# Recurrent heads of a hybrid decoder step: two chain links per round, the prompt's group normalisation in the later rounds, the state products on four row groups

## What is computed

```python
def step(st, inp):
    r_t, w_t, k_t, v_t, kk_t, b_t = inp
    sa = jnp.einsum('bhvk,bhk->bhv', st, -kk_t)
    st = st * w_t[:, :, None, :] + sa[..., None] * b_t[:, :, None, :] + v_t[..., None] * k_t[:, :, None, :]
    return st, jnp.einsum('bhvk,bhk->bhv', st, r_t)
st_final, ys = lax.scan(step, state0.astype(F32), xs)
y = jnp.swapaxes(ys, 0, 1)
mean = jnp.mean(y, axis=-1, keepdims=True)
var = jnp.mean(jnp.square(y - mean), axis=-1, keepdims=True)
y = ((y - mean) * lax.rsqrt(var + RWKV_GN_EPS)).reshape(B, S, RWKV_WIDTH)
y = y * gn_g.astype(F32) + gn_b.astype(F32)
bonus = jnp.sum(rf * kf * r_k.astype(F32), axis=-1, keepdims=True) * vf
out = ((y + bonus.reshape(B, S, RWKV_WIDTH)) * g.astype(F32)).astype(p.dtype)
```

## Time and profile before

| | us |
|---|---|
| time, median of 3 runs | 2107.24 (2105.16 to 2107.76) |
| span of the profiled execution | 2100.0 |
| the same execution with what lies around its span, taken as the median | 2107.24 |
| PE busy | 1898.0 (90%) |
| DVE busy | 704.1 (34%) |
| ACT busy | 510.4 (24%) |
| rounds of the recurrent heads | 431.53 to 497.79 |
| tail of the recurrent heads | 497.79 to 525.51 |
| next block's first transfer | 526.72 |

### The profile page before, as it was taken

The page is one execution under the profiler, slowest core; times in us unless marked ns, Lnnn a source line. Parts: engine busy times, 40 slices in busy tenths (PEclk is TensorE's granted clock), DMA queues, the critical chain, the costliest instruction groups (busy, mean ns, idle before and its releaser), DMA issues. The chain is left out here.

```text
span 2100.0 us, 38294 instructions
## 1 busy us (share of the span) xinstructions
PE 1898.0 (90%) x15868; PEld 1287.9 (61%) x15868; DVE 704.1 (34%) x1349; ACT 510.4 (24%) x861; POOL 139.8 (7%) x180
## 2 busy tenths in 40 slices
PE   6999996798879989989897999999999999999993
PEld 6999985766565558978644554544554554455441
DVE  4447758323535544446433111111111111111111
ACT  4446632232122223254222111101110111111111
POOL 0000000400023310000100000000000000000000
PEclk8999997788899999999997999999999999999997
DMA  8545531111233429524669999999999999999996
GB/s 225 142 126 134 140 74 23 24 41 28 108 104 108 136 76 290 141 101 126 231 272 372 415 422 424 427 423 395 407 423 426 421 423 404 409 424 422 422 426 217
DMA packets 210765, 543.62 MB, mean 259 GB/s; under 512 B 44536, under 2 KB 168538, under 8 KB 183632
## 3 DMA queue, kind: packets, MB, share of 16 engines
q1 hardware_dynamic: 202274, 532.97, 66.7%
q0 software_dynamic: 7936, 8.68, 2.0%
q10 hardware_dynamic: 438, 0.32, 0.1%
HBM read 524.86 MB, written 28.59 MB: 264 GB/s over the span
## 5 line engine op out<-in xcount | busy, mean ns | idle before, releaser
L2774 PE MATMUL p_u<-w_expert,xgT 128*64 128x256 f32 x2048 | 241.4, 390 | 32.5 <-DMA w_expert<-in_w_up_dram 32.4
L2774 PE MATMUL p_g<-w_expert,xgT 128*64 128x256 f32 x2048 | 231.9, 379 | 0.9 <-DVE xgT L2854 0.9
L2774 PEld LDWEIGHTS p_u<-w_expert,xgT 128*64 128x64 f32 x2048 | 149.3, 140 | 117.3 <-DMA w_expert<-in_w_up_dram 42.0
L2790 PE MATMUL p_y<-w_expert,hidT 128*64 128x512 f32 x960 | 219.2, 599 | 0.5 <-DVE hidT L2866 0.5
L2774 PEld LDWEIGHTS p_g<-w_expert,xgT 128*64 128x64 f32 x2048 | 147.2, 137 | 88.0 <-issue 18.8
L2742 PE MATMUL p_xg<-low,slot_sel 128*64 128x512 f32 x768 | 179.5, 603 | 5.2 <-DVE slot_sel L2838 5.2
L2790 PEld LDWEIGHTS p_y<-w_expert,hidT 128*64 128x64 f32 x960 | 66.7, 137 | 126.7 <-issue 125.9
L2859 DVE CAST row<-rowf 128x1 int32<-128x1 f32 x32 | 4.9, 154 | 357.4 <-POOLq L2949 357.4
L2909 ACT ACTIVATE act_g<-p_g 128x256 f32<-128x256 f32 x32 | 12.3, 384 | 429.6 <-PE p_u L2774 429.6
L2946 POOL DMA_INDIRECT x_dram<-y_slots,row x32 | 49.9, 1559 | 974.4 <-DVE y_slots L2870 974.4
L2742 PEld LDWEIGHTS p_xg<-low,slot_sel 128*64 128x64 f32 x768 | 52.9, 138 | 85.7 <-issue 75.4
(11 more groups left out here) (571 smaller groups left out, 2633.0 us busy)
## 6 DMA issues: line engine op xcount, KB each, us to landing
w_expert<-in_w_gate_dram SPq DMA_DIRECT2D x64, 2048.0 KB, 22.0
w_expert<-in_w_up_dram SPq DMA_DIRECT2D x64, 2048.0 KB, 23.2
w_expert<-in_w_down_dram SPq DMA_DIRECT2D x60, 2048.0 KB, 20.4
w_in_raw<-in_w_in_dram SPq DMA_DIRECT2D x32, 1024.0 KB, 5.7
lat<-in_cache_kv_latent_dram SPq DMA_DIRECT2D x128, 128.0 KB, 2.1
ho_raw<-in_w_out_dram SPq DMA_DIRECT2D x12, 1024.0 KB, 6.4
tables_sb<-in_w_out_dram SPq DMA_DIRECT2D x4, 1024.0 KB, 7.7
mem_k_s<-in_cache_mem_k_dram SPq DMA_DIRECT2D x8, 512.0 KB, 7.3
```

Source lines behind the costliest of these rows:

```text
L2774: mm = pe.matmul(acc[SL * h:SL * h + SL, 0:FF // 2], xgT[:, t, g // 2, :], w[g][:, FF * t + FF // 2 * h:FF * t + FF // 2 * h + FF // 2], s ...
L2790: mm = pe.matmul(p_y[SL * h:SL * h + SL, 512 * b:512 * b + 512], hidT[:, j, g, :], tile, start=(g == 0 and j == 0), stop=(g == 1 and j == 1))
```

## The change

1. **Two links per round.** `CHAIN` gives each round two links: round 0 has link 1, rounds 1 to 3 have links 2 and 3, 4 and 5, 6 and 7, and the later ones none. Each link's outputs go with it. The second link stands behind the outputs of the first, its outputs behind `states`.
2. **Normalisation spread.** From round 4 (`FIN_ROUND`) to round 7 each round normalises the prompt's 256 columns of two pairs (piece p = c - 4, 512 columns): `centre(p)` at the start of the round, `spread(p)` (sums of squares) before `states`, `inverses(p)` behind them. The transposes of the prompt's end state stand at the start of round 4. Piece 4, the samples' 64 columns of all eight pairs, is left for the tail.
3. **State products.** In `states` the four `b_exp` products (both n, both h) are issued first, then the four `k_exp` products, then the eight products with old states of n = 0 and of n = 1.
4. **Gates.** `gates(j)` makes the 320 columns of one pair; pairs 0 to 4 in rounds 1 to 5, 5 and 6 in round 6, 7 in round 7 (`GATES`).
5. ACT's eight additions of the bias (L1124) go in twos to rounds 0 to 3 instead of all to round 0. `cen` and `inv_g` become five buffers each. `head_uses` follows the new order.

The diff, cut:

```diff
+CHAIN = [(1, 0), (2, 3), (4, 5), (6, 7)] + [(0, 0)] * 5
+FIN_ROUND = 4
+GATES = [(), (0,), (1,), (2,), (3,), (4,), (5, 6), (7,), ()]
...
                     for n in range(2):
                         free(pe, ("st", j, n))
+                    for left, right in ((XS[:, :, 0:64], b_exp), (rowsS["v"], k_exp)):
+                        for n in range(2):
+                            for h in range(2):
+                                gg, hk = slice(64 * h + 32 * n, 64 * h + 32 * n + 32), slice(64 * h, 64 * h + 64)
+                                pe.matmul(B(("st", j, n))[hk, 0:288], left[gg, j, :], right[gg, j, :, :].rearrange("p b n -> p (b n)"), start=(right is b_exp), stop=False)
+                    for n in range(2):
                         empty_of(pe, "V", ("mts", j, n))
-                        for h in range(2):
-                            gg, hk = slice(64 * h + 32 * n, 64 * h + 32 * n + 32), slice(64 * h, 64 * h + 64)
-                            out = B(("st", j, n))
-                            pe.matmul(out[hk, 0:288], XS[gg, j, 0:64], b_exp[gg, j, :, :].rearrange("p b n -> p (b n)"), start=True, stop=False)
-                            pe.matmul(out[hk, 0:288], rowsS["v"][gg, j, :], k_exp[gg, j, :, :].rearrange("p b n -> p (b n)"), start=False, stop=False)
...
+                def gates(j):
+                    free(pe, ("gate", j))
+                    pe.wait_ge(g2_in, 16)
+                    for t in range(2):
+                        ins = pe.matmul(B(("gate", j))[:, 0:T], gate_w(t, j), sg[:, t, :], start=(t == 0), stop=(t == 1))
                     ins.then_inc(filled, 1)
+                def finals():
+                    empty_of(pe, "V", ("ch", NCH - 1))
...
+                def centre(p):
+                    free(pe, ("cen", p))
+                    if p == 4:
+                        empty_of(pe, "A", ("st", HP - 1, 1))
+                    else:
+                        empty_of(pe, "V", ("yp", NCH - 1))
+                    pe.matmul(B(("cen", p))[:, :], S.table("centre"), piece(y, p), start=True, stop=True).then_inc(filled, 1)
+                def spread(p):
+                    free(pe, ("gs", p))
+                    empty_of(pe, "A", ("cen", p))
+                    for e in range(8):
+                        ins = pe.matmul(B(("gs", p))[0:64, 2 * e:2 * e + 2], sqg[:, 512 * p + 64 * e:512 * p + 64 * e + 64], S.table("headsum")[:, 0:128:64], start=True, stop=True)
+                    ins.then_inc(filled, 1)
+                def inverses(p):
+                    free(pe, ("gi", p))
+                    pe.wait_ge(g_inverted, p + 1)
+                    for e in range(8):
+                        for h in range(2):
+                            ins = pe.matmul(B(("gi", p))[64 * h:64 * h + 64, 64 * e:64 * e + 64], inv_g[p][:, 2 * e + h:2 * e + h + 1].to_broadcast([64, 64]), ident[0:64, 0:64], start=True, stop=True)
+                    ins.then_inc(filled, 1)
                 for c in range(HP + 1):
-                    if 1 <= c < NCH:
-                        chain(c)
+                    first, second = CHAIN[c]
+                    p = c - FIN_ROUND if FIN_ROUND <= c < HP else None
+                    if c == FIN_ROUND:
+                        finals()
+                    if p is not None:
+                        centre(p)
+                    if first and c >= 1:
+                        chain(first)
                     if c < HP:
                         maps(c)
-                    if 1 <= c < NCH:
-                        outputs(c)
+                    if first and c == 0:
+                        chain(first)
+                    if first:
+                        outputs(first)
+                    if second:
+                        chain(second)
+                    if p is not None:
+                        spread(p)
                     if c >= 1:
                         states(c - 1)
+                    if second:
+                        outputs(second)
+                    if p is not None:
+                        inverses(p)
+                    for j in GATES[c]:
+                        gates(j)
+                centre(4)
+                spread(4)
+                inverses(4)
...
+                def squares(p):
+                    full_of(act, ("cen", p))
+                    done(act.activation(sqg[:, 512 * p:512 * p + 512], B(("cen", p))[:, :], ACT.Square))
+                def roots(p):
+                    full_of(act, ("gs", p))
+                    done(act.activation(inv_g[p], B(("gs", p))[0:64, 0:16], ACT.Sqrt, bias=gn_eps[:, :], scale=1.0 / HD))
...
+                def normalise(p):
+                    full_of(dve, ("gi", p))
+                    empty_of(dve, "V", ("cen", p))
+                    done(dve.tensor_tensor(cen[p], cen[p], B(("gi", p))[:, :], ALU.mult))
+                    dve.wait_ge(biased, HP)
+                    empty_of(dve, "V", ("gi", p))
+                    js = (2 * p, 2 * p + 1) if p < 4 else range(HP)
+                    ts = slice(0, SEQ) if p < 4 else slice(SEQ, T)
+                    for i, j in enumerate(js):
+                        x = cut(cen[p], p)[:, i, :]
+                        dve.scalar_tensor_tensor(x, x, S.vec('gn_g')[:, j:j + 1], k[:, j, ts], ALU.mult, ALU.add).then_inc(scaled, 1)
+                    empty_of(dve, "A", ("gate", js[-1]))
+                    dve.wait_ge(scaled, 2 * p + len(js))
+                    dve.tensor_tensor(piece(S.r, p), cut(cen[p], p), piece(gate, p), ALU.mult)
```

More of the change, by code:

```diff
@@ L1026, in _ @@
[L1026 to L1044, removed]
-                    for c, (o, w) in enumerate(CHUNKS):
-                        free(pe, ("gi", q, c))
-                        for e in range(o // 64, (o + w) // 64):
-                            for h in range(2):
-                                ins = pe.matmul(B(("gi", q, c))[64 * h:64 * h + 64, 64 * e - o:64 * e - o + 64], inv_g[q][:, 2 * e + h:2 * e + h + 1].to_broadcast([64, 64]), ident[0:64, 0:64], start=True, stop=True)
-                        ins.then_inc(filled, 1)
@@ L1253, in _, with link, output @@
-                normalise(0)
-                scale(0)
-                normalise(1)
-                scale(1)
+                def link(c):
+                    full_of(dve, ("ch", c))
+                    o = S.nn[:, c, :, :].rearrange("p j n -> p (j n)")
+                    done(dve.tensor_tensor(o, o, B(("ch", c))[:, :], ALU.add))
+                def output(c):
+                    full_of(dve, ("yp", c))
+                    o = y[:, :, CH * c:CH * c + CH]
+                    done(dve.tensor_tensor(o, o, B(("yp", c))[:, 0:256].rearrange("p (j t) -> p j t", j=HP), ALU.add))
@@ new lines, in _ @@
+                dve.wait_ge(mts_eye, 4)
+                for c in range(HP + 1):
+                    first, second = CHAIN[c]
+                    p = c - FIN_ROUND if FIN_ROUND <= c < HP else None
+                    if p is not None:
+                        hold(p)
+                    if first and c >= 1:
+                        link(first)
+                    if c < HP:
+                        for n in range(2):
+                            full_of(dve, ("mts", c, n))
+                            o = mts[:, c, 4 * n:4 * n + 4, :].rearrange("p b n -> p (b n)")
+                            done(dve.tensor_tensor(o, o, B(("mts", c, n))[:, 0:288], ALU.add))
+                    if first and c == 0:
+                        link(first)
+                    if first:
+                        output(first)
+                    if second:
+                        link(second)
+                        output(second)
+                    if p is not None:
+                        invert(p)
+                        normalise(p)
@@ L1259, in mla_project @@
+                hold(4)
+                invert(4)
+                normalise(4)
 def mla_project(nc, d, S, outs):
```

129 lines of the change are left out of this document (54 added, 75 removed).

## The result

| | before | after |
|---|---|---|
| time, median | 2106.2 us (4 runs) | 2085.77 us (2078.16 to 2086.61, 4 runs) |
| ratio, 95% interval | | 0.990 (0.9882 to 0.9917) |
| span of the profiled execution | 2100.0 us | 2076.5 us |
| time of the profiled execution | | 2078.16 us |
| rounds, from the first transpose of `maps(0)` to the start of the last old-state product | 66.1 us | 66.7 us |

The time lies 1.7 us under the range that was given, 7 us under the forecast. The interval of the ratio is 17.5 to 24.9 us of gain, where 14.2 were forecast. One difference matters later: 1.7 us lie between the span and the time of the changed kernel's profiled execution (2076.5 and 2078.16), not 7.24.

What follows compares the result with a forecast made beforehand. TensorE's instructions were taken to bound the rounds, a chain of dependent steps the tail. +13.9 - 9.2 - 18.9 = -14.2 us from the 2100.0 span gave 2085.8, plus 7.24 made 2093.0 us; range 2087.5 to 2099.5, extended to 2101.5 (0.82).

Steps and rivals of the forecast that it cites:

- The tail: After the last state product: one 512-column piece worked step by step, 8.8 us where 27.7 stood, 18.9 off; bounds 8.0 and 11.5.
- The cover for square, root and reciprocal: Rounds 4 to 7: TensorE's 2.3 us of centre and maps hide the square, 2.39 us of states hide root and reciprocal.
- rival B: Normalisation's chain shows in the rounds: TensorE stands some 2.5 us a piece, 10 us in all, 2103.0 us; chance 0.05.
- rival C: Handovers in rounds 4 to 7 bring the granted clock down: +26 us, 2119 us, slower than before; chance 0.05.
- The gates' price of 10.0 us: In the rounds: eight gates of 1280 columns at 8.6 us, with shape changes 10.0, as before; change 0 (-1 to +1).
- the time that lies around the span: Outside the profiled span: 7.24 us from span to median stay, taking 2085.8 to 2093.0 us.
- the links at 0: In the rounds: seven links and seven outputs are moved, none added, and the wait for the first link's add is covered: 0.
- the terms of the rounds: Rounds: 13.9 us on for normalisation, 9.2 off for state products, links and gates 0; they end 4.7 us later.
- state products, per pair: In `states`: four row groups and joined old-state products take 2.39 us where 3.54 stood, 9.2 us off for eight pairs.
- a piece of the normalisation: Rounds 4 to 7: centre, sums of squares and spread cost TensorE 3.27 us a piece, 13.1 for four.
- The bound of 10.2 us: State products' largest saving: 0.53, 0.59, 0.50 and 0.65 make 2.27 us a pair, 10.2 us off.
- nothing behind the block: After the block: nothing downstream is shorter, though the following block might gain up to 2 us from its start.

Runs made afterwards that it cites:

- the other order: Changed kernel with the four state products issued in the order h, n instead of n, h; the second four start 0.54 us after the first, 2.18 us a pair.

## Why the prediction was off

**What held.** The tail held: it took 8.8 us to DVE's last instruction in the first profile, as summed, and 29.1 to 29.6 us became 10.2 to 11.0 (forecast 18.9 off, measured 18.1 to 19.4). In the other three profiles of the changed kernel it is 0.8 us longer, because the last spread runs at the low level, a part of what the bound of 11.5 allowed for. The cover for square, root and reciprocal held, so rival B is out. The granted clock of rounds 4 to 7 was 1.00 in all four profiles, so rival C did not happen there. The gates' price of 10.0 us held too, and so did the view that a shorter block shifts all that follows.

**The step that failed first: the time that lies around the span.** I took 7.24 us, the distance from the profiled execution's span to the median of others, as lying around every execution alike. In every execution since it is 1.6 to 1.7 us (2078.16 against 2076.5, 2083.38 against 2081.7). So the profiled execution itself took some 2101.7 us, 5.5 less than the median, and my trace was of an execution that lacked a cost which most have. That cost is the long stretch at the low clock: rounds of 71.4 us in three of five profiles of the kernel before, 65.4 and 66.1 in the two others. The row for it stood in my list, the link at 1.97 us, but I used it for a rival and asked neither when the clock rises nor what precedes it.

**The second: the links at 0.** By the one trace, and as far as the clock goes, that was right. Against an execution with the stretch the links are worth 5 to 6 us, because the clock is up before the first state products. On average over the profiles of links alone (three) and of the kernel before (five) the block is 3.3 us shorter; the timed 2.7 us are not clear of none by themselves. The term was also put at nothing for what the new neighbours save, below.

**The third: the terms of the rounds**, nearly all too dear. Forecast +4.7 us for the rounds, measured +0.6 in the pair of profiles compared at first. Part of that pair's difference is luck, as the clock rose 1.5 us sooner in the one after than in the one before: on average the four profiles of the changed kernel have 67.6 us, and the two before without the stretch 65.8, +1.8.

| term | forecast | measured |
|---|---|---|
| state products, per pair | 2.39 | 2.28 (alone) |
| eight pairs | -9.2 | -10.1 by the rows, -10.2 in the block (alone) |
| a piece of the normalisation | 3.27 | 3.07 |
| end-state transposes and four pieces | +13.9 | +13.2 |
| gates, all | 10.0 | 10.0 (alone), 9.6 in the changed kernel |
| neighbours of one tile shape, without the gates | 0 | some -1.4 |

The state products were mis-sized by 0.9 us: the two sets of four take 0.54 and 0.59 where I gave 0.57 and 0.62, and the joined old states 1.15, not 1.20. The bound of 10.2 us that I called the far end held, barely. Larger is the last row, which the sum didn't have. I moved links, outputs, gates and pieces as if each kept its length. But a set is shorter before work of its own tile shape: the state products by 0.10 us before outputs (2.18 in place of 2.28) and 0.17 before a spread (475.49 to 477.60), the outputs by 0.10 before a link (0.95 and 1.05), a gate by 0.10 before a centre (1.18 and 1.28). By the rows the rounds come to 13.2 - 10.1 - 0.4 - 1.4 = +1.3 us, between the 0.6 and the 1.8 measured. One bound was added up wrongly: four pieces at 3.05 are 12.2, and the transposes' 0.8 belong to it, which makes the near bound 13.0 and the fast end of the range 2088.3.

The rule of the Trainium skill (TensorEngine Tiling (Array Packing), section Restrictions and Gotchas) that different row tiles cannot access the same PSUM bank at the same time is not borne out here: the second four matmuls start 0.53 us after the first, as after two, and 0.54 in the other order. My price for it was wrong too. The two matmuls of one n shared a bank in the kernel before as well, so by the rule it was they that would have run one after the other; their 0.53 us, the estimated length of one alone, already spoke against it.

**The fourth: nothing behind the block.** It was 1571.9 us on average of five profiles before (1570.4 to 1573.3) and 1570.3 of four after (1567.9 to 1572.0), so the 1.6 us between them are not clear of the scatter. 1.0 us of it is the output projection, which is steadier; its cause is open.

**Does it close?** The five profiles of the kernel before have blocks of 98.5 us on average, the four of the changed one 78.4: 20.1. With 1.6 behind the block it is 21.7 us; the medians of other executions gave 20.4 and 22.0. From my sum to it: 14.2, then 2.5 from the block in executions without the long stretch (95.1 against 78.4 is 16.7: rounds 2.9 cheaper than forecast, the tail 0.4 dearer), 3.4 for the stretch at its share of three in five, 1.6 behind. Block and rest make up these profiles' spans, so their sum must come out; the check is that it lies near the medians. Shares drawn from five and four profiles are rough, and the changed kernel's three times of 2085.56 to 2086.61 in the result, 2 to 3 us above its later profiles, have no profile of their own.

## What to carry to other kernels

Before a difference is added to a median, the profiled execution's own time belongs beside its span; if it is not near the median, its trace lacks something that most executions have, and a second and third profile are cheaper than a finer sum. A TensorE that is busy all the time can still run at half its clock, so the granted clock of each stretch is read together with which tile shapes run in it; in this kernel 64-row links and outputs placed ahead of 32-row state products went with the first of those products being paid at 2.4 GHz in all twelve profiles, where without them they were paid at 1.2 in five of eight. A term that is only moved is not a term of nothing: what stands beside it changes, and an experiment with one part alone, on the old neighbours, tells the two apart. A chain of small steps over several engines costs only TensorE's own part beside work that fills TensorE (3.07 us a piece here), and is worst at the end of a block, where it pays its latencies (4.8 us) and brings the clock down as well (7.3).

## What was not expected of the hardware

TensorE busy 5.00 of 5.00 us for three stretches in a row at a granted clock of 0.50 to 0.58 (436 to 451 us), with the same instructions at 1.00 in other executions of the same kernel. Four matmuls of 288 columns on four row groups in two banks take 0.53 us to the next four, as long as two on two row groups. And a chain through three engines costs 4.8 us a piece at the full clock, 7.3 at half.
